# Raw float32 weights for part of the first stage of a float32 transformer block: small columns, first convolution job and three quarters of the second

## The reference, cut to what matters

```python
c_act = silu(c)
mod = c_act @ w_ada + b_ada                     # w_ada is 2048 x 12288
sh_a, sc_a, gt_a, sh_f, sc_f, gt_f = split(mod, 6)
h = rmsnorm(x, norm_mix) * (1 + sc_a) + sh_a
p = h @ w_in                                    # 2048 x 9296
c_q, c_kv, k_pe, q_g, k_g, v_g, z, b_logit, a_logit, gate_logits = split(p)
```

## Time and profile before

| | |
|---|---|
| median of three runs | 2272.47 us (2271.64 to 2272.55) |
| the profiled execution | 2270.37 us, of which the span of its core is 2269.0 us |
| PE busy | 2191.9 us (97%) |
| DVE busy | 1512.9 us (67%) |
| ACT busy | 999.8 us (44%) |
| HBM read | 503.56 MB, 223 GB/s over the span |
| mean granted TensorE clock | 0.989 |

### The profile page before, as it was taken

How to read it: one execution, slowest core, us unless ns; L and a number is a source line. 1 busy time by engine, 2 the same in 40 slices (tenths; PEclk the granted TensorE clock), 3 DMA queues, 4 the chain that set the end, 5 groups by cost and what they waited for, 6 DMA issues and landing times.

```text
span 2269.0 us, 27387 instructions
## 1 busy us (share of the span) xinstructions
PE 2191.9 (97%) x10608; PEld 1841.6 (81%) x10608; DVE 1512.9 (67%) x1898; ACT 999.8 (44%) x1263; POOL 28.9 (1%) x28
## 2 busy tenths in 40 slices
PE   6788999999998999999999999999999999999998
PEld 4678998788886788888888888887888888888886
DVE  7989888778867667765544555566556655655556
ACT  4355444433443464443344434456444444444444
POOL 0000000000000000000000000000000000000000
PEclk9899999999999999999999999999999999999999
DMA  9978747676899858986656556556666666566663
GB/s 361 403 260 241 253 151 268 216 252 221 268 320 263 291 199 275 297 248 214 195 189 191 190 194 191 190 192 194 194 188 194 186 195 193 184 192 191 192 190 127
DMA packets 261844, 507.87 MB, mean 224 GB/s; under 512 B 35274, under 2 KB 51410, under 8 KB 256850
## 3 DMA queue, kind: packets, MB, share of 16 engines
q1 hardware_dynamic: 261714, 506.14, 68.3%
HBM read 503.56 MB, written 2.51 MB: 223 GB/s over the span
## 4 chain that ended last, share of the span: by engine, by line
PE 81%; DVE 9%; issue 3%; DMA 3%; ACT 3%; SPq 0%; POOL 0%; DVEq 0%; ACTq 0%; POOLq 0%
PE bank L1183 24%; PE bank L1185 24%; PE bank L1184 24%; DVE WL L1951 3%; DVE RAW L1938 2%; PE bank L1128 2%; PE bank L1372 1%; DMA RAW<-in_w_o_dram 1%; PE bank L1195 1%; PE bank L1197 1%; PE bank L1196 1%; DVE A L1938 1%; ACT WH L1451 1%; DVE A L2133 1%; DMA RAW<-in_w_o_gdn_dram 0%
## 5 line engine op out<-in xcount | busy, mean ns | idle before, releaser
L1951 DVE TENSOR_TENSOR WL<-RAW,WH 128x1024 fp32r<-128x1024 f32 x715 | 867.6, 1218 | 597.8 <-ACT WH L1451 591.2
L1451 ACT CAST WH<-RAW 128x1024 fp32r<-128x1024 f32 x715 | 745.6, 1046 | 902.6 <-PE bank L1185 722.9
L1183 PE MATMUL bank<-WH,HTh 128*128 128x512 f32 x1916 | 756.4, 395 | 12.9 <-DVE WL L1951 12.3
L1184 PE MATMUL bank<-WL,HTh 128*128 128x512 f32 x1916 | 748.9, 391 | 0.0
L1185 PE MATMUL bank<-WH,HTl 128*128 128x512 f32 x1916 | 748.7, 391 | 0.0
L1183 PEld LDWEIGHTS bank<-WH,HTh 128*128 128x128 f32 x1916 | 361.8, 189 | 90.1 <-DVE WL L1951 16.5
L1185 PEld LDWEIGHTS bank<-WH,HTl 128*128 128x128 f32 x1916 | 361.5, 189 | 76.5
L1184 PEld LDWEIGHTS bank<-WL,HTh 128*128 128x128 f32 x1916 | 361.8, 189 | 72.7
L1183 PE MATMUL bank<-WH,R2h 128*128 128x512 f32 x408 | 161.7, 396 | 5.9 <-DVE WL L1951 5.9
L1185 PE MATMUL bank<-WH,R2l 128*128 128x512 f32 x408 | 159.9, 392 | 0.0
L1184 PE MATMUL bank<-WL,R2h 128*128 128x512 f32 x408 | 159.8, 392 | 0.0
(11 more groups left out here) (280 smaller groups left out, 1816.0 us busy)
## 6 DMA issues: line engine op xcount, KB each, us to landing
RAW<-in_a_w_in_dram SPq DMA_DIRECT2D x192, 512.0 KB, 3.6
RAW<-in_w_gate_up_dram SPq DMA_DIRECT2D x176, 512.0 KB, 4.5
RAW<-in_w_in_dram SPq DMA_DIRECT2D x129, 512.0 KB, 5.2
RAW<-in_w_ada_dram SPq DMA_DIRECT2D x128, 512.0 KB, 5.8
RAW<-in_w_down_dram SPq DMA_DIRECT2D x88, 512.0 KB, 4.3
RAW<-in_a_w_out_dram SPq DMA_DIRECT2D x64, 512.0 KB, 3.8
A<-in_w_ada_dram SPq DMA_DIRECT2D x18, 1024.0 KB, 8.2
RAW<-in_w_o_dram SPq DMA_DIRECT2D x32, 512.0 KB, 6.4
```

Of the source, the lines that this page charges most:

```text
L1183: e.matmul(o, ah[:, s], hi[:, k, :], start=first, stop=False)
L1184: e.matmul(o, ah[:, s], lo[:, k, :], start=False, stop=False)
L1451: e.copy(hi, rv).then_inc(S["hi"], 1)
L1951: e.tensor_tensor(lo, rv, hi.bitcast(F32), ALU.subtract).then_inc(S["lo"], 1)
```

## The change

Seven things change.

1. On the host, w_in's columns for the front stage are laid out anew (`first_weights`): w_cs has, for each kt, 464 columns (`CS`): three column blocks of conv 1 (384) and the 80 small columns; w_cq has the 512 of cq; w_cd has ckv and conv 0 side by side (1024 columns); w_ct has the fourth column block of conv 1. Each is stored so that one partition's data of a unit is contiguous.
2. PE multiplies w_cs ("cs") and the conv 0 half of w_cd ("cf") as raw float32 against `tmp1`: one float32 matmul of 128x256 for each kt and column block, no halves. cs takes four for a kt (into banks 4 and 5), cf four (banks 6 and 7). The sm job and the splits of conv 0 go.
3. Job conv 1 keeps one column block, in two units of eight kt.
4. A unit of w_cd holds its raw slot until cf has used it. w_cs has two buffers of its own.
5. The front's order of steps is new: "h" of a group comes after the next group's first ada, and then PE has cs, cq, ckv, cf. There are six units in a group of two kt: ada, cd, ada, ada, ada, cq. The squares and the scaling of x change engines (scaling is all on ACT, in four pieces), and the rotary tables are spread over later steps.
6. The latents' transposes use banks 6 and 7, the small columns' bank 1, and the small columns' rest runs as one generator.
7. `BESIDE`: conv 1 loses its three half columns of `mod`, conv 2 four of six, uqn 0 and 1 one each; conv 3 and conv 4 gain two each, ga 2 two, each z job one, gb 3 one.

```diff
+
+CS = 3 * P + 80
...
-    def ba(t0, nkt, dst):
-        w = a["w_in"].rearrange("(t p) n -> p t n", p=P)
-        return [(dst[:, :, 0:64], w[:, t0:t0 + nkt, O_KPE:O_KPE + 64]),
-                (dst[:, :, 64:80], w[:, t0:t0 + nkt, O_BA:O_BA + 16])]
+    def laid(name):
+        return lambda t0, nkt, dst: [(dst, a[name][:, t0:t0 + nkt, :])]
...
-    front = [Job("sm", 0, ba, 16, 80, "ht", side="ch", lazy=True),
-             Job("cq", 0, plain(win, O_CQ), 16, 512, "ht", lazy=True),
-             Job("ckv", 1, plain(win, O_CKV), 16, 512, "ht", lazy=True),
-             conv(0, O_Q)]
+    front = [Job("cq", 0, laid("w_cq"), 16, 512, "ht", lazy=True),
+             Job("ckv", 1, laid("w_cd"), 16, 512, "ht", lazy=True),
+             Job("conv", 0, laid("w_cd"), 16, 512, "ht", side="ch", lazy=True)]
     for j in front:
         j.extra = EXTRA_R
-    a1 = [conv(1, O_Q + 512), conv(2, O_K)]
+    a1 = [Job("conv", 1, laid("w_ct"), 16, P, "ht", side="ch", step=8, lazy=True), conv(2, O_K)]
...
-BESIDE |= {("conv", 1): (3, 5, 7), ("conv", 3): (3, 7), ("conv", 4): (3, 7), ("conv", 5): (3, 7), ("ga", 2): (), ("gb", 3): (1, 3, 5),
-           ("wo", 0): (0, 1, 2, 4, 5, 6), ("wo", 1): (0, 1, 3, 5), ("gate", 0): ()}
+BESIDE |= {("conv", 1): (), ("conv", 2): (3, 7), ("uqn", 0): (1,), ("uqn", 1): (1,),
+           ("conv", 3): (1, 3, 5, 7), ("conv", 4): (1, 3, 5, 7), ("conv", 5): (3, 7), ("ga", 2): (3, 7), ("gb", 3): (1, 3, 5, 6),
+           "z": (1, 2, 3, 4, 6, 7), ("wo", 0): (0, 1, 2, 4, 5, 6), ("wo", 1): (0, 1, 3, 5), ("gate", 0): ()}
...
-        sm, cq, ckv, conv = jobs[:4]
+        cq, ckv = jobs[:2]
         last = ()
-        for k0, n in GROUPS:
+        for gi, (k0, n) in enumerate(GROUPS):
             g = [("g", 16 + k0 + k) for k in range(n)] + [("g", k0 + k) for k in range(n)]
             u.append(g[0])
             if last:
                 u.append(("w", ckv) + last)
-            u.append(g[1])
-            if last:
-                u.append(("w", conv) + last)
-            u.extend(g[2:])
             last = (k0, n)
-            u.extend([("w", sm) + last, ("w", cq) + last])
-        u.extend([("w", ckv) + last, ("w", conv) + last])
+            if gi + 1 == NG:
+                u.extend([("w", cq) + last, ("w", ckv) + last] + g[1:])
+            else:
+                u.extend(g[1:] + [("w", cq) + last])
         self.start_units = len(u)
-        order = [(j, t0) for j in jobs[4:] for t0 in range(0, j.nkt, j.step)]
+        order = [(j, t0) for j in jobs[3:] for t0 in range(0, j.nkt, j.step)]
...
+            if u[0] == "w" and u[1].name == "cq":
+                self.put("load_cs", group_of(u[2]))
             self.put("load", i, free)
...
-        sm, cq, ckv, conv = jobs
-        for gi, (_, n) in enumerate(GROUPS):
+        m = self.ms()
+        for n in range(4):
+            if n == 3:
+                self.put("x_sq", 1)
+                self.put("x_rs", m)
+            self.put("c", n)
+            if n == 0:
+                self.put("x_sq", 0)
+        self.put("x_sc", m)
+        self.put("xt")
+        cq, ckv = jobs[:2]
+        for gi, (k0, n) in enumerate(GROUPS):
+            self.front_ada()
             if gi:
-                self.front_half(sm, 2)
+                self.put("h", gi - 1)
+                self.put("cs", gi - 1)
                 self.front_half(cq, 0)
-            else:
-                m = self.ms()
-                self.put("x_sq", m)
+                self.front_split(ckv)
+                self.front_half(ckv, 1)
+                self.put("cf", gi - 1)
+            if gi == 2:
                 self.put("rope_tables")
-            for k in range(2 * n):
-                self.ada(self.staged[0], self.units[self.staged[0]][1])
-                self.issue_loads()
-                if gi and k == 0:
-                    self.front_split(ckv)
-                elif gi and k == 1:
-                    self.front_half(ckv, 1)
-                    self.front_split(conv)
-                elif k == 0:
-                    self.put("x_sc", m)
-                elif k == 1:
-                    self.put("xt")
-            if gi:
-                self.front_half(conv, 3)
+            if gi + 1 == NG:
+                self.front_split(cq)
+                self.front_split(ckv)
+            while self.ga_n < 2 * (k0 + n):
+                self.front_ada()
             self.put("cam", gi)
-            self.front_split(sm)
-            self.front_split(cq)
-            self.put("h", gi)
-        self.front_split(ckv)
-        self.front_split(conv)
+            if gi + 1 < NG:
+                self.front_split(cq)
+        self.put("h", NG - 1)
         self.put("load_cst2")
-        self.front_half(sm, 2)
+        self.put("cs", NG - 1)
+        self.fill(1)
+        self.put("smt")
         self.front_half(cq, 0)
         lat = [self.done(cq, 0), self.done(ckv, 1)]
-        self.fill(1)
-        next(lat[0])
-        self.fill(1)
         next(lat[0])
         self.front_half(ckv, 1)
         self.fill(1)
-        next(lat[0], None)
         next(lat[1])
-        self.front_half(conv, 3)
+        next(lat[0])
+        self.put("cf", NG - 1)
         self.fill(1)
-        self.pending[1] = lat[1]
-        self.bg.append(lat[1])
+        next(lat[1])
+        self.bg += lat
         self.have |= {("ht", kt) for kt in range(16)}
+
+    def front_ada(self):
+        self.ada(self.staged[0], self.units[self.staged[0]][1])
+        self.issue_loads()
 
     def front_split(self, j):
         i = self.staged[0]
         self.place.append(place)
...
-RAW1_FREE = (("lo", 4 * NG), ("ga_dve", 32))
+RAW1_FREE = (("lo", 2 * NG), ("ga_dve", 32), ("cs", 2 * NG))
...
+def conv_bank(L, n, q, i, pr):
+
+    if n == 1:
+        b = (5, 5, 4, 2 * pr)[2 * q + i]
+        return L.bank[b][:, 0:T] if (q, i) in ((0, 0), (1, 1)) else L.bank[b][:, T:2 * T]
+    return L.bank[2 * pr + q][:, i * T:(i + 1) * T]
...
+        elif kind == "cs":
+            gi, = args
+            k0, n = GROUPS[gi]
+            W.wait_ge(f"cs_in{gi % 2}", 16 * (gi // 2) + 16)
+            W.wait_ge("xmod", k0 + n)
+            for k in range(n):
+                w = L.CS[gi % 2][:, CS * k:CS * k + CS]
+                h = L.tmp1[gi % 2][:, k * T:k * T + T]
+                first, last = k0 + k == 0, k0 + k == 15
+                e.matmul(bank[4][:, T:2 * T], w[:, 2 * P:3 * P], h, start=first, stop=last, skip_group_check=True)
+                e.matmul(bank[4][0:80, 0:T], w[:, 3 * P:CS], h, start=False, stop=last, skip_group_check=True)
+                e.matmul(bank[5][:, 0:T], w[:, 0:P], h, start=first, stop=last, skip_group_check=True)
+                i = e.matmul(bank[5][:, T:2 * T], w[:, P:2 * P], h, start=False, stop=last, skip_group_check=True)
+            i.then_inc(S["cs"], 1)
+            held[4] = held[5] = [("cv_d", 24)]
+
+        elif kind == "cf":
+            gi, = args
+            k0, n = GROUPS[gi]
+            i = sch.cd_unit[k0]
+            W.wait_ge(f"raw{sch.raw_slot(i)}", sch.raw_value[i])
+            W.wait_ge("xmod", k0 + n)
+            if gi == 0:
+                take(6)
+                take(7)
+            for k in range(n):
+                w = L.raw(sch.raw_slot(i), n, 1024)[:, k, 512:1024]
+                h = L.tmp1[gi % 2][:, k * T:k * T + T]
+                first, last = k0 + k == 0, k0 + k == 15
+                for cb in range(4):
+                    o = bank[6 + cb // 2][:, (cb % 2) * T:(cb % 2) * T + T]
+                    t = e.matmul(o, w[:, cb * P:cb * P + P], h, start=first and cb % 2 == 0, stop=last, skip_group_check=True)
+            t.then_inc(S["cs"], 1)
+            held[6] = held[7] = [("cv_d", 12)]
...
         elif kind == "sm_t":
             W.wait_ge("smt", 1)
-            for bb in range(2):
-                i = e.transpose(bank[4][:, 80 * bb:80 * bb + 80], L.SMT[0:80, bb * P:bb * P + P], ident[0:80, 0:80])
+            W.wait_ge("lat_c", 2)
+            for bb in range(2):
+                i = e.transpose(bank[1][:, 80 * bb:80 * bb + 80], L.SMT[0:80, bb * P:bb * P + P], ident[0:80, 0:80])
             i.then_inc(S["sm_t"], 1)
-            held[4] = [("rope", 12), ("b_tanh", 2), ("dt_y", 2)]
...
                 W.wait_ge(*extra_free(sch, sch.place[hid]))
             e.copy(hi, rv).then_inc(S["hi"], 1)
 
...
         elif kind == "x_sc":
             W.wait_ge("rsq", args[0])
-            e.activation(L.XS1[:, 0, :], L.X[:, 0, :], ACT.Copy, scale=L.rs1[:, 0:1]).then_inc(S["xs"], 1)
+            for h in range(2):
+                hs = slice(1024 * h, 1024 * h + 1024)
+                for b in range(2):
+                    e.activation(L.XS1[:, b, hs], L.X[:, b, hs], ACT.Copy, scale=L.rs1[:, b:b + 1]).then_inc(S["xsq"], 1)
 
...
+            W.wait_ge("cs", 2 * gi - 2)
             for kt in range(k0, k0 + n):
                 e.activation(L.tmp1[gi % 2][:, (kt - k0) * T:(kt - k0 + 1) * T], L.XT0[:, kt, :], ACT.Identity,
...
         kind, args = step[0], step[1:]
 
```

(83 more changed lines are left out.)

94 lines of the change are left out of this document (39 added, 55 removed).

## The result

The changed kernel takes **2283.36 us** (median of 4 runs, 2279.58 to 2289.7) beside 2272.51 us for the kernel before: ratio 1.005, 95% interval 1.0038 to 1.0062. It is slower by half a per cent; 2258 us (2247 to 2270) had been predicted. The profiled execution is the slowest of its four (2289.7 us, span 2288.4), so a sum over its stages explains 19.3 us against the profiled execution before, not 10.9. The profiled executions of the experiments lie within 6 us of their medians.

A forecast was written before the change was run, and what follows sets the result against it. PE was busy 97% of the span, the front bound by DVE and DMA together. Off PE -17.3, front +3, relief -3, crowding +3 gave -14.3 us: a median of 2258 us, range 2247 to 2270.

The forecast's parts named there:

- +3 for the front: Front stage: its last matmul would end near 145.5 us, not 142.7; +3 us, bounds -3 and +10.
- fits, if the clock is up: Front: PE's burst per group of two kt takes 12.2 of 14.5 us, so it fits at full clock.
- 0.1 over today: Front: the loop over cd's slot takes 29.2 us for two groups, 14.6 each; 14.8 chosen from 14.5 to 15.6.
- The last groups: Front's end: a last group in which PE has 12.2 + 2 x 6.1 us queued, within the +3 us.
- Off PE after the front, -17.3: Conv 1 loses three of four column blocks, 144 matmuls of 0.12 us: -17.3 us, the term that pays.
- Relief -3, crowding +3: Behind the front: less DVE work may close PE's gaps, -3 us; evictions, latents' transposes and moved half columns crowd, +3 us.
- DMA and short clock dips: Rival, front: new layouts bring nothing, bursts sometimes start at low clock; +11 in place of +3, 2266 us; chance 0.2.
- PE at half clock: Rival, front: bursts take 24.4 us, SP stands behind late cf, a group takes 20.7; +39, 2297 us; chance 0.07.
- The estimated 2264: Rule against the change: at an HBM limit of about 358 GB/s the front's extra 3.1 MB cost 8.8 us.
- What would show it: Signs: right if raw pairs are 0.43 us apart; wrong if the front ends after 153 us or PE idles over 5.

The follow-up runs named there:

- e1: The changed kernel with cf right behind cs, ahead of cq and ckv, in each front group; 2275.84 us, ratio 1.0015.
- e11: The changed kernel without conv 0's raw products in the front, four unit-matrix multiplications per group standing in; 2278.39 us, ratio 1.0022.
- e2: The changed kernel with the latents' transposes alternating over banks 6 and 7; 2280.29 us, ratio 1.004.
- e5: The changed kernel with the key part's two transposes in idle bank 5 in place of bank 6; 2278.19 us, ratio 1.0034.
- e6: The changed kernel with the edits of e1 and e5 together; 2270.21 us, ratio 1.0001.
- e8: e6 with the old list BESIDE put back but for two entries (conv 1 and ga 2); 2272.37 us, ratio 1.0009.
- e3: The changed kernel with the last group's ada blocks loaded ahead of cq and cd, and cd split behind cs; 2287.38 us, ratio 1.0072.
- e10: e6 plus e2's edit, with cf also ahead of cs, first in each burst; 2275.56 us, ratio 1.0011.
- e4: The changed kernel with the edits of e1, e2 and e3 together; 2283.67 us, ratio 1.0049.
- e9: e6 plus e2's edit, with the latents' transposes two half steps later and the gates one later; 2270.13 us, ratio 0.9982.
- e12: e9 and e10 together; 2272.64 us, ratio 0.9997.

## Why the prediction was wrong

**The step that failed: "+3 for the front".** It measured +16.1 in the profile explained here, +9.7 and +13.0 in two others of the same front. Of its parts:
- *A burst of 12.2 us "fits, if the clock is up".* At full clock it is 12.4, nearly as computed. But PE waited before six of the nine bursts (21.6 us, up to 4.5), and four of the seven long ones took 14.4 to 15.5. I had put slow starts into a rival and reckoned the forecast's loop at full clock. The loop's other part, computed as 17.0, measured 17.0 in the turn shown; the whole was 31.6, not 29.2. As the rows read, loop and clock feed each other: held loads make DVE late, DVE makes PE idle, idleness makes the next burst slow, and its cf, last in it, frees the slot later. What the slow starts cost without the hold, and the hold without them, no run separates.
- *A loop "0.1 over today", 14.8 a group chosen.* That is near what a group takes with the hold shortened or gone (15.0 in e1 and e11), where DMA bounds it. I had chosen 14.8 for its nearness to the loop, so that it met DMA's floor is partly luck. With the hold it was 15.9.
- *The last groups.* I added PE's queue, but not that the last ada block reuses a slot which cf of group 6 frees. From the first ada of group 7 (counted from 0, at 123.77) to the last ada is 20.6 us, before 11.4: 9 of the 16 us (in e2 and e5 18.2 and 20.1).
- A row was misread too. The matmul at 142.57 us, which I took for conv 0's last, is the 24th of conv 1: the front before ended at 139.8. A "+3" means 142.8, which e1 (143.5) and e11 (143.2) come near.

**"Off PE after the front, -17.3".** The matmuls went: conv 1 took 6.0 us in place of 33.8, which held 8.7 us of lost time as well. So the term was right; that the stretch to conv 3 shrank by only 7.0 us lies with the jobs behind conv 1.

**"Relief -3, crowding +3".** DVE's busy time fell as said, 104.1 to 84.6 us in 143 to 255 us, and no gap closed for it. Crowding was three things. The latents' transposes stood in PE's queue before results that DVE had yet to make (conv 2 lost 18.9 us, before 3.5). This I had named, but at +3. The key part's copy held bank 6 for 9 us; my step said nothing of where the small columns' rest, now one generator and later, meets the next taker of its bank. The list BESIDE seems to cost 8 us at conv 3 to 5 and og and wo, by one profile each of e6 and e8, where I had looked at DVE's share alone; it gave 6 back right behind the front, so e8, with the old list, was no faster.

**Rivals.** "DMA and short clock dips" was near the truth in the clock dips but had no price for the hold: 2266; and its layouts that bring nothing did not come true. "PE at half clock" named the loop with SP behind it and its side; its 2297 needed whole bursts at half clock. The section "HAM oscillation — how this bites in real kernels" of the Trainium skill's page "TensorE: Matmul & The Clock Gate", by which waits between bursts start each one at the low clock, agrees here with the rows at 91.91 and 124.45 us, and not with the burst at 75.86, which came after 3.2 us of waiting and started near full speed. The estimated 2264 by the limit in the Trainium skill's "DMA: Bandwidth & Descriptors", section "Specifications", was nearer to the measured 2283 than mine, but for a wrong reason: the front ran at up to 421 GB/s, well above 358.

**What would show it** served well: raw products at full clock were 0.43 us apart (four of cs in 1.73 us, 107.42 to 109.15), and a front end after 153 us, SP waiting for cf with DVE idle, and over 5 us of idleness before the latents' transposes (5.05 us at 170 us) all came.

Not tried: undoing conv 1's move alone, so its share in the final gain is inferred from the stages; keeping PE busy between the bursts, which would have told the clock from the hold; and e3's order with w_ct in a slot that cf does not hold.

## What to carry to other kernels

When a tile slot's last reader changes from a fast engine to the last step of a long PE burst, walk the loop "slot free, load, vector work, burst, slot free" with the burst at the clock that it has after the wait which the loop itself makes, and walk it through the last groups as well. Put the work that frees a slot early in the burst, as long as nothing else waits for what it displaces (e1 and e10). Look as well at the first load of the next stage: if it reuses the slot that is freed last, it stands outside (7 us of PE in e3 and e4). And when small work is moved later, look for who takes its PSUM bank next: here one bank was worth 5.5 us of the stretch behind the front (e5) and a few half steps of order 2.6 (e9), together as much as 67 matmuls of 0.12 us.

## What the runs showed of the hardware that I had not expected

- The front's loads moved at 421 GB/s with a DMA share of 1.02 (the changed kernel, 66 to 102 us), where they had moved at 403 with a share of 1.03. The trace's packets in that window show where the difference lies: before, 2020 of 2048 bytes took 88 ns each, 1239 of 8192 bytes 318 ns, and 1243 of 64 and 256 bytes 11 and 18 ns; after, those of 4096 bytes took 160 ns, those of 8192 bytes 313 ns, and the small sizes are gone. A byte in a packet of 2048 was a tenth dearer than in one of 4096, and the very small packets took 18 us of the 16 engines' 576.
- A burst slowed by its start costs little by itself (2 to 3 us), but it lies in a loop that DMA and DVE close: taking PE's 24 half products out of that loop gave 7.5 us, though PE was idle for 11 and 18% of the two windows of the front.
- One profile can mislead by as much as the effect. The ten executions of e1 spread over 8.6 us, those of e12 over 9.9, and the kernel before over 3.5 to 6.7 on the same chips; the front of the changed kernel ended at 149.5, 152.8 and 155.9 in three profiles.
